# In-projection groups 7 to 15 of the second half in seven products instead of eight

## The reference, cut to what matters

```python
for l in range(DEPTH):
    h = _rmsnorm(x, norm_gain[l])
    proj = jnp.einsum('bsd,de->bse', h, w_in[l])
    q, k, v, g_attn, x_rnn, g_rnn = jnp.split(proj, splits, axis=-1)
    attn = _swa_sink_attention(q, k, v, sinks[l], cos, sin)
    xc = _causal_conv(x_rnn, conv_w[l], conv_b[l])
    rnn = _rg_lru(xc, w_rgate[l], b_rgate[l], w_igate[l], b_igate[l], lru_param[l])
    mixed = jnp.concatenate([attn * jax.nn.silu(g_attn), rnn * jax.nn.silu(g_rnn)], axis=-1)
    x = x + jnp.einsum('bse,ed->bsd', mixed, w_out[l])
return _rmsnorm(x, final_gain)
```

## Time and profile before

| what | value |
|---|---|
| median of 3 runs | 2303.87 us (2301.64 to 2306.47) |
| the profiled execution | 2304.23 us, its span 2301.7 us |
| PE busy | 2292.8 us (100%), 13798 products |
| DVE busy | 1565.0 us (68%) |
| ACT busy | 1339.1 us (58%) |
| DMA engines, queue of SP | 38.1% of the span, 259.91 MB |
| DMA engines, queue of POOL | 4.5%, 25.17 MB |
| chain that ended last | PE 96%, of it plain products (L682) 80%, narrow (L703) 10% |

### The profile page before, as it was taken

One profiled execution on the slowest core, in us unless ns is written; L12 is line 12 of the kernel. 1 busy time (PEld: TensorE's weight loads), 2 busy tenths in 40 slices (PEclk: granted clock), 3 DMA queues, 4 the chain that ended last, 5 costly groups with the idle time before them and its releaser, 6 DMA issues.

```text
span 2301.7 us, 36298 instructions
## 1 busy us (share of the span) xinstructions
PE 2292.8 (100%) x13798; PEld 1919.3 (83%) x13798; DVE 1565.0 (68%) x2546; ACT 1339.1 (58%) x2564; POOL 32.3 (1%) x58
## 2 busy tenths in 40 slices
PE   9999999999999999999999999999999999999999
PEld 8877888899888888889888888888988888888898
DVE  7658868656646877856675786885565478778555
ACT  7557666445546857645564676763455557666444
POOL 1110000000000000000000000000000000000000
PEclk9999999999999999999999999999999999999999
DMA  8886334545333233344534333344543333333444
GB/s 259 237 243 174 88 92 120 152 138 139 96 93 98 86 89 92 96 145 139 163 110 152 111 95 89 96 139 138 142 131 96 97 91 86 93 92 96 117 136 152
DMA packets 141389, 287.48 MB, mean 125 GB/s; under 512 B 16416, under 2 KB 20768, under 8 KB 138784
## 3 DMA queue, kind: packets, MB, share of 16 engines
q1 hardware_dynamic: 138096, 259.91, 38.1%
q0 software_dynamic: 2688, 25.17, 4.5%
q10 hardware_dynamic: 432, 0.10, 0.0%
HBM read 276.73 MB, written 33.55 MB: 135 GB/s over the span
## 4 chain that ended last, share of the span: by engine, by line
PE 96%; DVE 2%; DMA 1%; ACT 1%; issue 0%; DVEq 0%; POOL 0%; ACTq 0%; POOLq 0%
PE proj L682 80%; PE proj L703 10%; PE ps_at L811 2%; DMA wall<-in_w 1%; PE ps_at L786 1%; PE ps_at L830 1%; PE proj L722 1%; ACT wcut L905 0%; DVE wcut L1307 0%; PE proj L749 0%; PE ps_at L640 0%; DVE mixed L1791 0%; DVE acc L1402 0%; ACT operand L942 0%; PE ps_at L764 0%
## 5 line engine op out<-in xcount | busy, mean ns | idle before, releaser
L682 PE MATMUL proj<-operand,wcut 128*128 128x512 f32 x8376 | 1944.0, 391 | 1.3 <-DVE xr L1558 1.3
L682 PEld LDWEIGHTS proj<-operand,wcut 128*128 128x128 f32 x8376 | 1563.7, 188 | 337.9 <-issue 10.3
L1307 DVE TENSOR_TENSOR wcut<-wall,wcut 128x512 fp32r<-128x512 f32 x871 | 600.1, 689 | 582.0 <-ACT wcut L905 575.1
L905 ACT ACTIVATE wcut<-wall 128x512 fp32r<-128x512 f32 x870 | 548.3, 630 | 547.2 <-DMA wall<-in_w 381.0
L703 PE MATMUL proj<-xsum_out,wcut 128*128 128x256 f32 x1104 | 136.8, 283 | 0.0
L703 PEld LDWEIGHTS proj<-xsum_out,wcut 128*128 128x128 f32 x1104 | 134.9, 192 | 0.6
L703 PEld LDWEIGHTS proj<-operand,wcut 128*128 128x128 f32 x828 | 105.3, 191 | 3.9 <-DVE proj L1371 0.3
L703 PE MATMUL proj<-operand,wcut 128*128 128x256 f32 x828 | 106.6, 283 | 0.0
L1011 ACT ACTIVATE gy<-proj 32x512 f32<-32x512 f32 x144 | 85.1, 591 | 26.6 <-PE proj L682 22.1
L1102 ACT ACTIVATE sqr<-ps_at,pars 64x512 f32<-64x512 f32 x64 | 43.9, 685 | 91.8 <-PE ps_at L830 91.4
L1063 ACT ACTIVATE prob<-ps_at,stat 128x128 f32<-128x128 f32 x256 | 90.1, 363 | 0.8
(11 more groups left out here) (173 smaller groups left out, 1520.6 us busy)
## 6 DMA issues: line engine op xcount, KB each, us to landing
wall<-in_w SPq DMA_DIRECT2D x710, 256.0 KB, 2.6
wall<-weight_sums SPq DMA_DIRECT2D x92, 256.0 KB, 2.7
weight_sums<-in_blocks POOLq DMA_DIRECT2D x36, 512.0 KB, 6.5
wall<-in_blocks SPq DMA_DIRECT2D x69, 256.0 KB, 2.6
x<-in_xt SPq DMA_DIRECT2D x16, 512.0 KB, 3.8
mixed<-in_xt SPq DMA_DIRECT2D x14, 512.0 KB, 6.7
weight_sums<-weight_sums POOLq DMA_DIRECT2D x12, 512.0 KB, 5.2
gw<-in_gates SPq DMA_DIRECT2D x32, 128.0 KB, 2.6
```

Source lines behind the costliest of these rows:

```text
L682: last = pe.matmul(bank_of(l, 2 * g + m)[:, :], wcut[:, n % RING, a, c:c + P], operand[:, k, b, :], start=(i == 0 and k == 0), stop=(k == ...
L905: act.activation(wcut[:, u % RING, 0, :], wall[:, u % RING, 1, :], ACT.Copy).then_inc(w_hi, 1)
L1307: dve.tensor_tensor(wcut[:, u % RING, 1, :], wall[:, u % RING, 1, :], wcut[:, u % RING, 0, :].bitcast(F32), ALU.subtract).then_inc(w_lo, 1)
```

## The change

In-projection groups 7 to 15 go into the scheme of seven products in the second half, in both layers. With that, 18 groups have 11 units instead of 8; in the first half the same groups take four of their eight units from the blocks of weights, at the same number of products. POOL's sums grow from six batches to sixteen. They are built in three stretches: batches 0 and 1 at the start, 2 to 8 after slot 132 of the first layer of the first half, 9 to 15 after slot 132 of the second. x of layer 1 in the second half goes to DRAM in slots 1 to 4, since the operand sums take its place, and is reloaded from slot 127 on.

```diff
-IN_SEVEN = {(0, 0): (), (0, 1): (), (1, 0): (), (1, 1): ()}
+IN_SEVEN = {(0, 0): (), (0, 1): (), (1, 0): range(7, IN_LAST + 1), (1, 1): range(7, IN_LAST + 1)}
...
+OPENS = {2: (0, 0, 132), 9: (0, 1, 132)}
...
                 if before:
                     copy(S4, n - 1, S2)
+                if n in OPENS:
+                    pool.wait_ge(built[S4], 32 * n - 16)
+                    add(S4, n - 1, A12)
+                    pool.wait_ge(unit_done, at_unit(*OPENS[n]))
                 if now:
...
-                if before:
+                if before and n not in OPENS:
                     pool.wait_ge(built[S4], 32 * n - 16)
                     add(S4, n - 1, A12)
```

## The result

The changed kernel takes 2348.85 us (2336.04 to 2357.95, 4 runs) against 2302.76 (2301.56 to 2306.47, 4 runs) of the kernel before: ratio 1.0193, 95% interval 1.0144 to 1.0243. The direction was forecast, the size was not: 2312 was said, 2330 was the upper end. The profiled execution is the slowest of the four, 2357.95 us with a span of 2356.2.

The account below looks back on a forecast made before the run. PE was taken as the bound, busy 2292.8 of 2301.7 us. The sum was 2304.2 - 13.9 (PE work) - 2.8 (start) + 13 (DVE and ACT) + 10 (sums) + 1.5 (rest) = 2312.0; forecast 2312, range 2296 to 2330 us.

Parts of the forecast that it names:

- The weight sums: GpSimd's sixteen batches: start relieved, -2.8 us; second part, late weight loads in the first half's output stages, +10 us (2 to 24).
- upper bound of 24 us: Top of the +10 us for the output stages: each of eight queues holds PE for 3 us, 10.9 less 7.2.
- 3.2 to 4.5 us to spare: Slack of a weight load in stages with narrow units, after 2.7 us of landing and 1.3 of splits.
- Rival (4): The DMA queues saturate and each burst costs 3 us: 2328 us, chance 0.12.
- The PE work: Second half, groups 7 to 15 in both layers: 0.77 us less per group, 18 groups, -13.9 us.
- DVE and ACT: Second half, groups 7 to 15: added splits and lead sums make DVE the bound in heavy groups, +13 us (4 to 23).
- the rest: Operand sums in the second half and x of layer 1 going out and back: 0 to 4 us, taken as +1.5.
- the walk: Times followed through group 9 of the second half: PE waits 0.5 us; a heavy group after a heavy one costs 2.3.
- The start: First layer, 107.64 to 244.08 us: fewer sums beside the attention, 136.44 us becomes 133.66, -2.8 us.
- What would show it: Signs: cycles of 26 to 27 us in groups 8 and 9, output cycles over 21.0, landings after 5 us or more.

Follow-up runs that it names:

- last_three: small_front8 with only groups 13 to 15 of the second half in seven products, ten batches of sums instead of sixteen; 2295.2 us, ratio 0.9964.
- no_in_sums: The changed kernel without the ten new batches; narrow units of the in-projection groups read blocks of the weights instead of sums; 2303.4 us, ratio 1.0001.
- small_front8: The changed kernel with batches 0 to 7 at the start, 8 to 15 from slot 8 of the first half's second layer, rows of 2 KB; 2302.6 us, ratio 0.9996.
- sums_alone: The changed kernel with no in-projection group in seven products; all sixteen batches are built, the ten added ones never used; 2345.3 us, ratio 1.0184.

## Why the prediction was wrong

**The term that failed** is "The weight sums", second part: "together 1.05 ... GpSimd has no deadline and gives way in part, so I take +10 us". The place and the mechanism were right: four output cycles of the first layer grew from 21.0 us to between 27.4 and 29.3, and those of the second layer to up to 27.1, behind late weight loads. The term measured 53.1 us in the profiled execution and some 44 in the median one, where +10 was said. Three steps of its size were wrong.

1. I put 0.55 and 0.50 together, treated the excess of 0.05 as time to be shared, and let POOL give way. It does not. From 445 to 565 us it moved 17.14 MB, and in the kernel before, beside the plain stage from 45 to 165 us, 16.94 MB (the line below); a batch takes 29 us in both places. The weights moved 12.95 MB instead of 16.32. The excess was the wrong measure in any case: the two queues together held 0.89 of the engines while PE waited.

```profile
q0 software_dynamic: 1813, 16.94, 58.2%
```

2. The upper bound of 24 us counted eight bursts of 3 us. By the prediction's own 3.2 to 4.5 us to spare on top of 2.7, a narrow unit bears a landing of 5.9 to 7.2 us; I took the 7.2 and a longest landing of 10.9, read beside a plain stage. Beside the output stage 25 of 50 loads and, in the second layer, 14 of 52 took over 7.2 us. PE's timeline has 15 waits there, eight of them of 2.5 to 4.6 us, 34.1 us in all: ten above my upper bound before anything else is counted.
3. I had no price for what follows a wait: the 19.0 us of products that took longer, some 15.5 of them at a granted clock of 0.50, all of that behind waits of 3 us and more. Nothing in the trace before showed this, since PE has no wait of a microsecond in it past its start; that was a reason for a wider range above.

Rival (4) named the mechanism, saturated queues, and gave 2328, still 21 us short, by reasons 2 and 3.

**The PE work**, -13.9: the direction was right and the size too small. In last_three a group in seven gives 0.93 us net of everything else, which would be 16.8 us for 18 groups.

**DVE and ACT**, +13 with +1.5 for the rest: the net of it and the PE work was +0.6 by my sum, and no_in_sums has -0.3 by its medians (+2.4 for the second half by the marks). The place was half right. By the marks of the first layer, with a gain of 0.93 us set against each group, group 7 costs 0.5 us, group 8 4.8 (it grew by 3.9), group 9 0.8, groups 10 and 11 together 1.4 and group 12 1.9, where the walk had 0.5, 2.3, 2.3, 0.6 and 0.5. The wait in group 8 is for a PSUM bank, which has no term in the prediction. My walk through the splits of group 9 foresaw a wait of 0.5 us before the third late and one of 0.9 before the first plain unit after it: PE shows 0.43 and 0.53. It then put 2.3 us on such a group, more than its own splits gave, which didn't happen in group 9. That the sum came out is partly luck: a gain that was too small by 3 us stood against costs that were too small by 2 us (by the medians) to 5 (by the marks).

**The start**, -2.8: exactly as said, 133.67 us for 136.44. Another 1.7 us were lost before 107.64 us, and the first marks of the other kernels differ there by -0.6 to +0.9 without a change that would explain it.

**What would show it**: output cycles over 21.0 us and landings over 5 us came (medians of 7.1 and 5.3); the cycles of 26 to 27 us in groups 8 and 9 did not both come (the interval that holds group 8 is 29.4 us, the next 25.4).

## What to carry to other kernels

Before background transfers are set beside a stage, take from the trace how long that stage can wait for a load, and count the loads that took longer beside the same transfers; neither the busy share of the DMA engines nor the median landing tells it. Here each load over 7.2 us went with 1.2 to 1.4 us lost. Place the transfers beside the stage with the longest lead, cut them into short rows and let them pause; each of these alone gave back 35 to 39 of the 46 us. And let a cheaper scheme reach only the groups that have room on the other engines: three groups in seven per layer beat nine by 7 us (last_three against small_front8).

## What the runs showed of the hardware

**Row length against another queue's delay.** At some 13.3 MB of POOL's transfers in 120 us, rows of 2 KB cost PE 3.5 us where the kernel's rows of 8 KB and more cost 12.5, at a DMA share of 0.92 and 0.88. That is the second layer, in one execution of each; the median landing there is 4.4 against 4.6 us and the longest 9.3 against 9.5, but 4 of 61 loads took over 7.2 us with short rows and 10 of 56 with long ones.

**A background queue that does not give way.** POOL's queue moved 17.14 MB in 120 us beside the output stage and 16.94 MB beside a plain stage, 58.0% and 58.2% of the engines' time, while SP's weights beside that output stage fell from 16.32 MB to 12.95.

**The clock behind a wait.** Past the first 30 us and before the last 25 of the kept traces, seven waits of 3.1 to 4.6 us and one of 3.0 each stand beside a stretch of 3 to 10 us in which the granted clock is 0.50; another wait of 3.02 us (sums_alone, 1047.79 us) has the full clock behind it. After waits of 1.7 us and less the clock stayed full. Between, at 1.8 to 2.8 us, it can go either way. These are the two layers of small_front8, nearly the same wait in each (2.31 and 2.29 us), by the table of stretches right behind it:

```profile
1351.00:1353.00 2.00, 1.76 (x13) 1.71 (x14) 1.93 (x6) 1.47 (x3) 0.00 (x0) 1.00 0.23 24
```

```profile
1922.00:1924.00 2.00, 2.00 (x12) 2.00 (x12) 1.97 (x4) 1.90 (x3) 0.00 (x0) 0.57 0.52 139
```

By the marks group 8 grew by 2.4 us in the first layer and by 3.8 in the second, so the same wait costs 1.4 us more with the slow products behind it.
